# Expert gate and up weights loaded and awaited in two halves of four row blocks

## The chip, the cores and the metric

The kernel runs on one core of a Trainium2 chip. The metric is device time in microseconds (us) of one execution of the whole program. Three executions of the kernel before gave 1589.13, 1584.79 and 1586.37 us; the median is 1586.37.

## What is computed

Two layers of a backbone with two streams of 128 tokens each (context and latent), 1024 wide, all in float32. Each layer has a token-mixing part (gated linear attention, a convolution module and neighbourhood attention, joined by an output projection) and a mixture-of-experts part, the one that the change touches:

```python
scores = jax.nn.sigmoid((t @ router_w).astype(jnp.float32))
...
top_e = lax.top_k(masked, TOP_K)[1]                # 8 of 64 experts for each token
...
act = jax.nn.silu(jnp.einsum('td,edf->tef', t, w_gate)) * jnp.einsum('td,edf->tef', t, w_up)
routed = jnp.einsum('tef,efd->td', act * gate[:, :, None], w_down)
```

An expert has a gate and an up matrix of 1024 x 256 and a down matrix of 256 x 1024, 1.049 MB each. The 256 tokens together reach all 64 experts, so a layer loads 192 such matrices.

## The kernel before, in words

**Passes.** The experts of a layer are ordered by load and packed into 26 passes (`WIDTHS`, lines 90 to 92; `PLACED`, line 111). A pass fills 128 token rows with four tiles of 32; an expert takes one to four of them, so a pass serves one to four experts and a layer's 26 passes serve 64. The loop over layers runs this stage twice.

**Slots and loads.** Five slots in the on-chip memory hold one expert each (four in `ring`, one in `store` and `work`, lines 431 to 435). SP, the engine that issues these transfers, goes through the passes in order (lines 560 to 573). For each expert of the pass it reads the expert's number, waits in `gate_up_free` until the slot's gate and up part is free (for all but the first five experts: until `gu_done` counts the pass that used it last), and issues two transfers (`load_gate_up`, lines 437 to 440), gate and then up. Both count on the slot's semaphore `gate_in`, 16 each. Then, for each expert of the pass, it waits in `down_free` until `Y_shown` counts the second down half of the slot's last pass and issues the down matrix (`load_down`, `down_in`). All of it is one queue in order: what stands behind a waiting issue waits too.

**Layout.** Partition p of a slot holds the eight consecutive rows 8p to 8p+7 of each matrix, 256 floats a row (`"(p k) n -> p k n"`, k = 8), gate first and then up. A row block kt is the 128 rows 8p+kt.

**TensorE (PE).** For each pass p (lines 987 to 1012) PE

1. waits for `gate_in` of all experts of the pass (lines 990, 991) and for the gathered tokens (`X_kept`, line 992);
2. runs `gate_up_pass` (lines 936 to 941): for kt from 0 to 7 and for each of the four tiles a product of 32 columns of `X_e` with 512 columns of weights (gate and up of row block kt), added up in bank 4; the last one counts `gu_done`;
3. scatters the rows of the pass before (`scatter`, line 965), turns this pass's weights and activations (lines 946, 952), gathers half of the next pass's tokens (`gather`, line 925);
4. waits for `down_in` of all experts of the pass and for `turn_kept`, runs the first half of the down products (line 958), gathers the other half of the tokens and runs the second half.

Each float32 product appears as two instructions, so `gate_up_pass` shows 64 a pass. ACT takes the gate half through Silu (line 1239) as soon as `gu_done` counts, VectorE multiplies it with the up half (line 1543), and ACT copies the turned activations (line 1241), the tokens of the next pass (line 1224) and so on.

Of the kernel before, what the change touches and what calls it, by code (L numbers as in the profile page):

```python
# [26 lines left out]
KT = D // P  # L27
# [32 lines left out]
SLOTS = len(EXPERT_SLOTS)  # L60
# [61 lines left out]
first_done first_kept first_bias""".split()  # L122

SIGNALS = """matrices bias_next small_in vec_in norm_in attn_in shared_in chunk_in0 chunk_in1 chunk_in2
gate_in0 gate_in1 gate_in2 gate_in3 gate_in4 down_in0 down_in1 down_in2 down_in3 down_in4 act_step dve_step ada_done ada_kept bias_in square_done 
mod_shown h_ready hT_shown hT_ready vec_shown vec_ready proj_done proj_kept z_shown la_log la_ready
conv_sig tap conv_ready convT_shown ctok_ready convB_shown conv_neg cact_ready pw_shown cat_conv nq_ready
kco_ready nT_shown nT_ready bias_ready scores_shown max_ready p_exp p_ready pT_shown pT_ready pv_shown cat_na
# [17 lines left out]
def expert_slot(e):  # L146
    return EXPERT_SLOTS[e % SLOTS]


def build(nc, A):  # L150
# [4 lines left out]
    s = {name: nc.alloc_semaphore(name) for name in LASTING + SIGNALS}  # L155
# [265 lines left out]
    def dma_in(eng, out, in_, sem):  # L421
        eng.dma_start(out, in_).then_inc(sem, 16)

    def pre_slot(n):
        return n % PRE_SLOTS
# [5 lines left out]
    def slot_gate_up(slot):  # L431
        return ring[:, slot, 0:2 * KT * FF] if slot < RING else slot4_gate_up
# [4 lines left out]
    def load_gate_up(eng, slot, weights, sem):  # L437
        for j, w in enumerate(weights):
            dma_in(eng, slot_gate_up(slot)[:, KT * FF * j:KT * FF * (j + 1)].rearrange("p (k n) -> p k n", k=KT),
                   w.rearrange("(p k) n -> p k n", k=KT), sem)  # L440

    def load_down(eng, slot, w, sem):
        dma_in(eng, slot_down(slot).rearrange("p (j n) -> p j n", j=2), w.rearrange("(p j) n -> p j n", j=2), sem)

# [18 lines left out]

    chunk_in = [s["chunk_in0"], s["chunk_in1"], s["chunk_in2"]]
    gate_in = [s["gate_in0"], s["gate_in1"], s["gate_in2"], s["gate_in3"], s["gate_in4"]]
    down_in = [s["down_in0"], s["down_in1"], s["down_in2"], s["down_in3"], s["down_in4"]]
    N_SMALL, N_VEC, N_ATTN = 18, 8, 2 * HEADS + 2

    layers = nc.Fori(0, DEPTH)
    layer = layers.__enter__()  # L470
    following = (layer + 1) % DEPTH
    with nc.Block() as block:
        @block.sync
        def _(sp):
            dma_in(sp, gbc[:], A["norm_mix"][bass.ds(layer, 1), :].partition_broadcast(P)[:, 0, :], s["norm_in"])

            for n in range(PRE):
                if n >= PRE_SLOTS:
                    chunk_used(sp, n - PRE_SLOTS)
                slot = ring[:, pre_slot(n), :]  # L480
                sem = chunk_in[pre_slot(n)]
# [78 lines left out]
            for p in range(PASSES):  # L560
                wave = [k for k in range(EXPERTS) if EXPERT_PASS[k] == p]
                e = {}
                for k in wave:
                    r = LOADED[k][1]
                    e[k] = sp.value_load(order_i[0:1, r:r + 1], min_val=0, max_val=EXPERTS - 1)
                    gate_up_free(k)
                    load_gate_up(sp, expert_slot(k),
                                 [A[w][layer, bass.ds(e[k], 1)][0] for w in ("exp_w_gate", "exp_w_up")],
                                 gate_in[expert_slot(k)])
                for k in wave:  # L570
                    down_free(k)
                    load_down(sp, expert_slot(k), A["exp_w_down"][layer, bass.ds(e[k], 1)][0],
                              down_in[expert_slot(k)])
# [42 lines left out]
        def _(pe):  # L616
# [63 lines left out]
            for c in range(2):  # L680
                last = nc.tensor.transpose(bank(5, 64 * c, 64 * c + R_END), vec[:, P * c:P * (c + 1)],
                                           ident[0:R_END, 0:R_END])
# [12 lines left out]
            for st in range(STREAMS):  # L695
                for c in range(2):
                    at = 256 * st + P * c
                    last = nc.tensor.transpose(bank(4, at, at + P), cacc[:, c, st, :], ident[:])
# [8 lines left out]
            for a in range(PAIRS):  # L707
                last = nc.tensor.transpose(bank(1, P * a, P * (a + 1)), kvc[:, 0, P * a:P * (a + 1)], ident[:])
# [5 lines left out]
            for c in range(2):  # L714
                for st in range(STREAMS):
                    at = 256 * c + P * st
                    last = nc.tensor.transpose(bank(5, at, at + P), cTok[:, st, P * c:P * (c + 1)], ident[:])
# [4 lines left out]
            for e in range(2):  # L722
                r = slice(DK * e, DK * (e + 1))
                for a in range(PAIRS):
                    last = mm(bank(e, P * a, P * (a + 1)), qnT[r, a, 0:P], knT[r, a, 0:P], start=True, stop=True)
            last.then_inc(s["scores_shown"], 1)
            for e in range(2):
                r = slice(DK * e, DK * (e + 1))
                for a in range(PAIRS):
# [3 lines left out]
                    last = mm(bank(2 + e, 256 * a + P, 256 * (a + 1)), qnT[r, a, P:2 * P], kcT[r, a, :],  # L733
                              start=True, stop=True)
# [4 lines left out]
            for o in range(2):  # L739
                for c in range(2):  # L740
                    last = mm(bank(4, 256 * o, 256 * (o + 1)), wpw[:, c, P * o:P * (o + 1)],
                              cacc[:, c, :, :].rearrange("p s t -> p (s t)"), start=(c == 0), stop=(c == 1))
# [6 lines left out]
            for i, block_in in enumerate(blocks):  # L749
                last = nc.tensor.transpose(bank(1 + i // 4, P * (i % 4), P * (i % 4 + 1)), block_in, ident[:])  # L750
# [54 lines left out]
            for e in range(2):  # L805
                for a in range(PAIRS):
# [6 lines left out]
                    last = mm(out1, kvc[:, 1, DK * hh:DK * (hh + 1)], pT[:, HEADS + 2 * i + 1, :],  # L813
                              start=False, stop=True)
# [115 lines left out]
            def tiles(p):  # L930

                k0 = EXPERT_PASS.index(p)
                return [(TILE * (first + i), expert_slot(k0 + c))
                        for c, (r, first, w) in enumerate(PLACED[p]) for i in range(w)]

            def gate_up_pass(b, tiles):
                for kt in range(KT):
                    for first, slot in tiles:
                        last = mm(ps[first:first + TILE, 4, :], X_e[:, b, kt, first:first + TILE],  # L939
                                  gate_up(slot, kt), start=(kt == 0), stop=(kt == KT - 1))  # L940
                return last
# [45 lines left out]
            for p in range(PASSES):  # L987
                q = p % 2
                used = [EXPERT_PASS.index(p) + c for c in range(len(PLACED[p]))]
                for k in used:  # L990
                    pe.wait_ge(gate_in[expert_slot(k)], 32 * (k // SLOTS + 1))
                pe.wait_ge(s["X_kept"], 2 * p + 2)
                gate_up_pass(q, tiles(p)).then_inc(s["gu_done"], 1)
                if p:
                    pe.wait_ge(s["Y_kept"], 2 * p)
                    scatter().then_inc(s["scattered"], 1)
                pe.wait_ge(s["S_ready"], p + 1)
                turn_weights()
                pe.wait_ge(s["act_done"], p + 1)
                turn_acts().then_inc(s["turned"], 1)  # L1000
                if p + 1 < PASSES:
                    pe.wait_ge(s["G_ready"], p + 2)
                    gather(6, G[1 - q], 0).then_inc(s["X_shown"], 1)
                for k in used:
                    pe.wait_ge(down_in[expert_slot(k)], 16 * (k // SLOTS + 1))
                pe.wait_ge(s["turn_kept"], p + 1)
                down_pass(tiles(p), 0).then_inc(s["Y_shown"], 1)
                if p + 1 < PASSES:
                    pe.wait_ge(s["X_kept"], 2 * p + 3)
                    gather(6, G[1 - q], 1).then_inc(s["X_shown"], 1)  # L1010
                pe.wait_ge(s["Y_kept"], 2 * p + 1)
                down_pass(tiles(p), 1).then_inc(s["Y_shown"], 1)
# [685 lines left out]
```

## Time and profile before

| what | value |
|---|---|
| median of three executions | 1586.37 us |
| the profiled execution, its own time | 1593.01 us |
| its span, first to last instruction | 1591.3 us |
| mean granted TensorE clock over the span | 0.966 of full speed |
| PE busy | 1463.2 us (92%) |
| HBM read | 505.49 MB, 319 GB/s over the span |
| weights of the experts, both layers | 384 transfers of 1024 KB |

The page gives times in microseconds. PE is TensorE's products, PEld its weight loads (which overlap the products), DVE is VectorE, ACT is ScalarE, SP the engine that issues most transfers. The span is also shown in 40 equal slices, with one digit for the busy share of each engine in tenths. A view of windows gives, for stretches of the span, the busy time and number of instructions of each engine, the granted clock of TensorE, the share of the 16 DMA engines that was busy (a little over 1 where packets overlap) and the rate. A row of the timeline gives the start, the duration, and in brackets the idle time before with what ended it. In the view of waits the columns are the total, the number of waits and the longest.

### The profile page before, as it was taken

To read this page: it belongs to the slowest core of one execution; us is meant where nothing else is said; L and a number is where in the kernel's file an instruction comes from. 1 tells how busy PE (TensorE), PEld (TensorE's weight loads), DVE (VectorE), ACT (ScalarE), POOL (GpSimd) and SP (SyncE) were. 2 spreads that over 40 slices of the span, in tenths; PEclk is the share of its full clock that TensorE was granted. 3 is DMA by queue.
4 is the path that set the end of the run, shared out by engine and by line. 5 is a ranking of instruction groups with operands and counts; after the bars stand their busy time and mean duration, and the time that the engine had idled before them with its cause. 6 is when DMAs were issued, how large, how long until landed. Compare 5 with 4: busy or idle time off the path is not lost. (4 is left out here: it accounts for less than half of the span.)

```text
span 1591.3 us, 28207 instructions
## 1 busy us (share of the span) xinstructions
PE 1463.2 (92%) x12120; PEld 781.4 (49%) x12121; DVE 459.7 (29%) x956; ACT 260.0 (16%) x441; POOL 107.1 (7%) x349
## 2 busy tenths in 40 slices
PE   4899989899999998999959999889999999999996
PEld 3665765644434443434436667564443444344442
DVE  2291784501111110111133639571111111111112
ACT  1223211511111110111113131041111111111110
POOL 2600430000000000000000016000000000000000
PEclk8999989899999999999989999989999999999999
DMA  7755960399999999999944678207999999999994
GB/s 252 257 181 190 334 218 1 134 421 420 421 421 406 400 422 397 421 420 420 374 158 137 245 260 309 87 1 327 421 420 416 421 421 420 419 400 421 419 421 178
DMA packets 109252, 509.56 MB, mean 320 GB/s; under 512 B 12864, under 2 KB 14652, under 8 KB 59196
## 3 DMA queue, kind: packets, MB, share of 16 engines
q1 hardware_dynamic: 108508, 506.52, 79.4%
q8 instruction: 100, 1.64, 0.4%
q0 software_dynamic: 384, 1.05, 0.2%
q14 instruction: 36, 0.29, 0.1%
q10 hardware_dynamic: 224, 0.06, 0.0%
HBM read 505.49 MB, written 2.10 MB: 319 GB/s over the span
## 5 line engine op out<-in xcount | busy, mean ns | idle before, releaser
L939 PE MATMUL ps<-ring,h 128*32 128x512 f32 x2720 | 375.4, 601 | 25.5 <-DMA ring<-in_exp_w_up 15.0
L939 PEld LDWEIGHTS ps<-ring,h 128*32 128x32 f32 x2720 | 110.3, 111 | 248.9 <-issue 248.9
L958 PE MATMUL ps<-ring,work 128*32 128x512 f32 x1360 | 199.6, 598 | 3.1 <-DVE store L1545 1.6
L939 PE MATMUL ps<-store,h 128*32 128x512 f32 x608 | 189.9, 615 | 9.0 <-issue 5.4
L965 PE MATMUL ps<-store,work 128*128 128x512 f32 x416 | 192.4, 605 | 1.6 <-DVE store L1553 1.6
L925 PEld LDWEIGHTS ps<-tm,work 128*128 128x128 bf16 x2496 | 144.4, 98 | 44.3 <-issue 43.1
L925 PE MATMUL ps<-tm,work 128*128 128x128 bf16 x2496 | 156.9, 219 | 0.3
L1543 DVE TENSOR_TENSOR work<-work,ps 128x256 f32<-128x256 f32 x52 | 21.9, 422 | 410.7 <-ACT work L1239 410.7
L965 PEld LDWEIGHTS ps<-store,work 128*128 128x128 f32 x416 | 74.7, 189 | 120.0 <-issue 116.5
L1545 DVE COPY store<-ps 128x512 f32<-128x512 f32 x52 | 36.0, 692 | 328.9 <-PE ps L958 328.9
L673 PE MATMUL ps<-ring,store 128*128 128x512 f32 (+1 forms) x256 | 101.3, 555 | 0.0
L958 PE MATMUL ps<-work 128*32 128x512 f32 x304 | 99.2, 598 | 0.0
L1239 ACT ACTIVATE work<-ps 128x256 f32<-128x256 f32 x52 | 20.0, 384 | 481.8 <-PE ps L939 481.8
L1224 ACT COPY h<-ps 128x512 f32<-128x512 f32 x104 | 61.0, 587 | 177.3 <-PE ps L925 177.3
L319 PE MATMUL ps<-ring,cs 128*32 128x128 f32 x1792 | 60.3, 291 | 17.7 <-DMA ring<-in_w_ada 17.7
L958 PEld LDWEIGHTS ps<-ring,work 128*32 128x32 f32 x1360 | 42.3, 109 | 69.4 <-issue 56.8
L622 PE MATMUL ps<-store,pick 128*128 128x128 f32 x384 | 54.1, 307 | 22.0 <-issue 10.2
L673 PEld LDWEIGHTS ps<-ring,store 128*128 128x128 f32 x256 | 49.3, 195 | 48.7 <-issue 46.8
L670 PE MATMUL ps<-store,ring 128*128 128x256 f32 (+1 forms) x288 | 66.9, 393 | 2.2 <-ACT store L1073 2.2
L939 PEld LDWEIGHTS ps<-store,h 128*32 128x32 f32 x608 | 47.7, 113 | 39.9 <-issue 39.9
L622 PEld LDWEIGHTS ps<-store,pick 128*128 128x128 f32 x384 | 52.8, 222 | 28.2 <-issue 22.1
L607 POOL TENSOR_TENSOR store<-h,work 128x64 f32<-128x64 f32 x196 | 57.2, 333 | 132.0 <-PE ps L813 95.4
(276 smaller groups left out, 1316.8 us busy)
## 6 DMA issues: line engine op xcount, KB each, us to landing
ring<-in_exp_w_gate SPq DMA_DIRECT2D x102, 1024.0 KB, 15.0
ring<-in_exp_w_up SPq DMA_DIRECT2D x102, 1024.0 KB, 17.2
ring<-in_exp_w_down SPq DMA_DIRECT2D x102, 1024.0 KB, 15.5
ring<-in_w_ada SPq DMA_DIRECT2D x28, 2048.0 KB, 10.4
store<-in_exp_w_gate SPq DMA_DIRECT2D x26, 1024.0 KB, 15.0
store<-in_exp_w_up SPq DMA_DIRECT2D x26, 1024.0 KB, 17.1
work<-in_exp_w_down SPq DMA_DIRECT2D x26, 1024.0 KB, 14.8
ring<-in_w_in SPq DMA_DIRECT2D x6, 2048.0 KB, 13.0
```

Of the source, the lines that this page charges most:

```text
L319: last = nc.tensor.matmul(out[32 * c:32 * (c + 1), :], cs[:, kt, :], w[:, kt, P * c:P * (c + 1)], start=(kt == 0), stop=(kt == KT - 1))
L607: last = tt(*views, ALU.mult)
L622: last = mm(bank(b, P * c, P * (c + 1)), pick[:, c, st, :], ada[:, n, :], start=True, stop=True)
L670: last = mm(ps[0:w, b, 0:STREAMS * P], wt[:, kt, :], hT[:, kt, :], start=(kt == 0), stop=(kt == KT - 1))
L673: last = mm(bank(b, 0, w), hT[:, kt, P * st:P * (st + 1)], wt[:, kt, :], start=(kt == 0), stop=(kt == KT - 1))
L925: last = mm(bank(X_bank, P * k, P * (k + 1)), hs[:, part, st, KT // 2 * half + k, :], onehot[:, st], start=(st == 0 and part == 0), stop=( ...
L939: last = mm(ps[first:first + TILE, 4, :], X_e[:, b, kt, first:first + TILE], gate_up(slot, kt), start=(kt == 0), stop=(kt == KT - 1))
L958: last = mm(ps[first:first + TILE, 7, :], turn[:, P * j + first:P * j + first + TILE], down(slot, j, half), start=(j == 0), stop=(j == 1))
L965: last = mm(bank(2 * st + half), turn[:, FF + P * st:FF + P * (st + 1)], Y[:, 512 * half:512 * (half + 1)], start=False, stop=False, skip_ ...
L1224: return nc.scalar.copy(X_e[:, b, KT // 2 * half:KT // 2 * (half + 1), :], bank(6).rearrange("p (k n) -> p k n", n=P))
L1543: tt(acts[:, 0, :], silu[:, 0, :], bank(4, FF, 2 * FF), ALU.mult).then_inc(s["act_done"], 1)
L1545: nc.vector.tensor_copy(Y[:, 0:512], bank(7)).then_inc(s["Y_kept"], 1)
```

## The change

`load_gate_up` of the routed experts is replaced by two calls of a new `load_part`, one for row blocks 0 to 3 and one for 4 to 7. An expert's gate and up matrices come in four transfers: gate first half, up first half, gate second half, up second half. The second halves count on five new semaphores, `rest_in`. `gate_up_pass` takes a range of row blocks; a pass waits for the first halves of all its experts, runs the products of blocks 0 to 3, waits for the second halves of all its experts, and runs blocks 4 to 7. The last product counts `gu_done` as before. The waits on `X_kept` move ahead of those on the weights. `load_down`, the slots, the order of experts, the shared expert and the path for left-over tokens stay as they were.

```diff
+    HALF_KT = (slice(0, KT // 2), slice(KT // 2, KT))
+
+    def load_part(eng, slot, weights, kts, sem):
+
+        for j, w in enumerate(weights):
+            dma_in(eng, slot_gate_up(slot).rearrange("p (a k n) -> p a k n", a=2, k=KT)[:, j, kts, :],
+                   w.rearrange("(p k) n -> p k n", k=KT)[:, kts, :], sem)
...
                     gate_up_free(k)
-                    load_gate_up(sp, expert_slot(k),
-                                 [A[w][layer, bass.ds(e[k], 1)][0] for w in ("exp_w_gate", "exp_w_up")],
-                                 gate_in[expert_slot(k)])
+                    for kts, half_in in zip(HALF_KT, (gate_in, rest_in)):
+                        load_part(sp, expert_slot(k),
+                                  [A[w][layer, bass.ds(e[k], 1)][0] for w in ("exp_w_gate", "exp_w_up")],
+                                  kts, half_in[expert_slot(k)])
...
-            def gate_up_pass(b, tiles):
-                for kt in range(KT):
+            def gate_up_pass(b, tiles, kts=range(KT)):
+                for kt in kts:
...
-                for k in used:
-                    pe.wait_ge(gate_in[expert_slot(k)], 32 * (k // SLOTS + 1))
                 pe.wait_ge(s["X_kept"], 2 * p + 2)
-                gate_up_pass(q, tiles(p)).then_inc(s["gu_done"], 1)
+                for kts, half_in in zip(HALF_KT, (gate_in, rest_in)):
+                    for k in used:
+                        pe.wait_ge(half_in[expert_slot(k)], 32 * (k // SLOTS + 1))
+                    last = gate_up_pass(q, tiles(p), range(kts.start, kts.stop))
+                last.then_inc(s["gu_done"], 1)
```

## Rows read from the trace of the kernel before

**Rows 1.** The page: busy time of the engines; then DMA in 40 slices.

```profile
PE 1463.2 (92%) x12120; PEld 781.4 (49%) x12121; DVE 459.7 (29%) x956; ACT 260.0 (16%) x441; POOL 107.1 (7%) x349
...
DMA  7755960399999999999944678207999999999994
GB/s 252 257 181 190 334 218 1 134 421 420 421 421 406 400 422 397 421 420 420 374 158 137 245 260 309 87 1 327 421 420 416 421 421 420 419 400 421 419 421 178
```

**Rows 2.** DMA view of the first expert stage, 305 to 790 us.

```profile
DMA packets 27605, 201.38 MB, mean 415 GB/s; under 512 B 3056, under 2 KB 3056, under 8 KB 3056
```

**Rows 3.** Timeline of PE in the first layer: starts of passes, the last pass.

```profile
377.71 0.60 PE L939 MATMUL ps<-ring,h 128*32 128x512 f32 x3
...
394.73 0.61 PE L958 MATMUL ps<-ring,work 128*32 128x512 f32 x3
...
395.15 7.05 PE L939 MATMUL ps<-ring,h 128*32 128x512 f32 x64
...
453.44 1.08 PE L939 MATMUL ps<-store,h 128*32 128x512 f32 x3 [3.57 <-issue]
...
784.35 0.63 PE L939 MATMUL ps<-ring,h 128*32 128x512 f32 x3 [1.09 <-DMA store<-in_exp_w_up]
...
796.28 0.63 PE L958 MATMUL ps<-ring,work 128*32 128x512 f32 x3 [0.77 <-ACT work L1241]
```

**Rows 4.** Waits of PE over the span: total us, times, longest us.

```profile
PE ps L939 <- DMA ring<-in_exp_w_up: 18.6, 8, 4.3
...
PE ps L939 <- issue: 13.5, 8, 3.6
```

**Rows 5.** Windows: stretches of the two expert stages; clock, DMA share, GB/s last.

```profile
513.00:519.00 6.00, 6.00 (x36) 2.20 (x29) 0.42 (x1) 0.38 (x1) 0.00 (x0) 1.00 0.75 289
544.00:550.00 6.00, 5.41 (x52) 2.06 (x56) 0.52 (x1) 0.00 (x0) 0.00 (x0) 1.00 0.86 315
620.00:628.00 8.00, 7.56 (x76) 2.54 (x71) 0.69 (x1) 0.13 (x1) 0.00 (x0) 1.00 0.81 302
...
1394.00:1402.00 8.00, 7.56 (x73) 2.54 (x76) 0.80 (x2) 0.59 (x1) 0.00 (x0) 1.00 0.85 308
...
792.00:794.00 2.00, 2.00 (x6) 0.84 (x5) 0.32 (x1) 0.00 (x0) 0.00 (x0) 1.00 0.14 57
...
450.00:460.00 10.00, 6.56 (x36) 1.86 (x40) 0.63 (x1) 0.00 (x0) 0.00 (x0) 0.66 1.02 423
```

**Rows 6.** DMA view of 16:24, 829:832, 46:49, 26:27, 390:430 us, in that order.

```profile
DMA packets 1519, 3.10 MB, mean 387 GB/s; under 512 B 17, under 2 KB 17, under 8 KB 1517
...
DMA packets 395, 1.21 MB, mean 404 GB/s; under 512 B 0, under 2 KB 0, under 8 KB 395
...
DMA packets 407, 1.25 MB, mean 417 GB/s; under 512 B 0, under 2 KB 0, under 8 KB 407
...
DMA packets 126, 0.40 MB, mean 401 GB/s; under 512 B 9, under 2 KB 9, under 8 KB 126
...
DMA packets 2308, 16.82 MB, mean 420 GB/s; under 512 B 258, under 2 KB 258, under 8 KB 258
```

**Rows 7.** DMA issues of the whole span: count, KB each, us to landing.

```profile
ring<-in_exp_w_down SPq DMA_DIRECT2D x102, 1024.0 KB, 15.5
...
ring<-in_sh_w_gate SPq DMA_DIRECT2D x2, 1024.0 KB, 6.2
```

**Rows 8.** Timeline of SP: two issues of one expert.

```profile
772.94 0.34 SPq L422 DMA_DIRECT2D store<-in_exp_w_gate  x1
773.37 0.38 SPq L422 DMA_DIRECT2D store<-in_exp_w_up  x1
```

**Rows 9.** Waits of SP over the span: total us, times, longest us.

```profile
SPq L422 <- PE ps L958: 332.8, 40, 9.0
SPq L422 <- PE ps L939: 331.6, 47, 14.2
```

More of the change, by code:

```diff
@@ L124 @@
 SIGNALS = """matrices bias_next small_in vec_in norm_in attn_in shared_in chunk_in0 chunk_in1 chunk_in2
-gate_in0 gate_in1 gate_in2 gate_in3 gate_in4 down_in0 down_in1 down_in2 down_in3 down_in4 act_step dve_step ada_done ada_kept bias_in square_done
+gate_in0 gate_in1 gate_in2 gate_in3 gate_in4 rest_in0 rest_in1 rest_in2 rest_in3 rest_in4 down_in0 down_in1 down_in2 down_in3 down_in4 act_step dve_step ada_done ada_kept bias_in square_done
 mod_shown h_ready hT_shown hT_ready vec_shown vec_ready proj_done proj_kept z_shown la_log la_ready
@@ L465, in build @@
     gate_in = [s["gate_in0"], s["gate_in1"], s["gate_in2"], s["gate_in3"], s["gate_in4"]]
+    rest_in = [s["rest_in0"], s["rest_in1"], s["rest_in2"], s["rest_in3"], s["rest_in4"]]
     down_in = [s["down_in0"], s["down_in1"], s["down_in2"], s["down_in3"], s["down_in4"]]
```

## The prediction, made before the changed kernel was run

> **What bounds the kernel now.** I read the page first. Over the span PE is busy 92%, but in the two long plateaus of the slices (the ninth to the 20th and from the 29th on, the expert stages of the two layers) the DMA line stands at 9 and the GB/s line near 420 in nearly every slice [rows 1]. Two engines near full: the question is which ends last. The traffic answers. One layer loads 64 experts of three 1.049 MB matrices, 201.3 MB, and the DMA view of the first stage, 305 to 790 us, counts 201.38 MB at a mean of 415 GB/s [rows 2]. The stage lasts as long as these bytes take. PE, by the timeline, needs 17.45 us for a pass that waits for nothing (377.71 to 395.15) [rows 3]: 26 passes are 453.7 us against 479.3 us for 201.3 MB at 420 GB/s. So the expert stage is bound by the weight stream, and PE sits out most of the difference ahead of line 939, 18.6 and 13.5 us over both layers [rows 4]. The 13.5 put to "issue" are of the same kind: the 3.57 us before 453.44 lie at the first product of a pass, where the gate wait stands [rows 3].
>
> The stream itself is nearly gapless. It runs dry in four places: 289 GB/s over 6 us, 315 over 6, 302 over 8, 308 over 8 [rows 5]. Against 420 that is 1.9 + 1.5 + 2.2 + 2.1 = 7.7 us of lost stream in both layers. There SP stood at a slot that PE had not freed. These 7.7 us are all that an earlier PE can win from the middle of a stage.
>
> **The change part by part.** *Earlier start of a pass (removes).* Of an expert's four transfers the last two carry 1.049 MB, 2.5 us at 420 GB/s. The 64 products of line 939 take 7.05 us [rows 3], so half of them (3.5 us) cover 2.5: a pass that waits today starts up to 2.5 us earlier and, if the stream is on time, waits no more in its middle. In a stream-bound stage this does not shorten the stage by 2.5 us a pass, since the next bytes come no sooner; what is late next is the next expert's weights. It wins in two places only. (a) Slots come free earlier, so the dry places shrink. Of 7.7 us I take 7, because the stream also gets slower (below), which lets PE catch up. (b) The last pass of a layer starts earlier against the end of the stream. Today it starts at 784.35, its down products start at 796.28 after ACT (line 1241), and the last bytes land between 792 and 794 [rows 3, 5]. About 2 us after that landing are all that can go, as the down products would then wait for down_in instead. Two layers: -4 us.
>
> *Smaller packets (adds).* A partition reads 8 rows of 256 floats, 8192 contiguous bytes, of each matrix; with half the row blocks it reads 4096. In 390 to 430 us the view counts 2308 packets, 258 of them small, so 2050 carry 16.82 MB: 8.2 KB each, 420 GB/s [rows 6]. No stretch has 4096 alone at length, so I bound its rate by neighbours in size. Column chunks of w_ada (2 KB) ran at 387 GB/s, of w_in (3 KB) at 404 in one stretch and 417 in another, a stretch mostly of the 4 KB rows of x at 401 [rows 6]. One engine's time for a packet is its bytes over a sixteenth of the rate: 84.7 ns (2048), 121.7 (3072 at 404), 117.9 (3072 at 417), 312.1 (8192). Lines to 8192 give for 4096: 160.5 ns (408 GB/s), 159.8 (410) and 156.7 (418). Gate and up are 134.2 MB a layer: 319.5 us at 420, 328.1 at 409, 321.1 at 418, 334.7 at 401. I take 409, because the two stretches behind it come after some microseconds of saturated queues, as the expert stage does, and 417 stands at the start of one: +8.6 us a layer, +17.2 in both. Ends: +3.2 and +30.4.
>
> The Trainium skill has a measured load stream of 1 MiB transfers with 4 KiB rows, 408.7 GB/s on a core alone (DMA: Bandwidth & Descriptors, iDMA fabric); with it the term would be +17.7, and no run here shows that stream yet.
>
> *More transfers (adds).* 128 more a layer. Each ends in one small packet per engine (3056 in 305 to 790 us for 192 transfers, 16 each) [rows 2]. The line from 2048 to 8192 has a constant of 84.7 - 75.8 = 8.9 ns a packet; 128 of them are 1.1 us a layer, +2.3 in both. Below: nothing, if it overlaps. Above: an idle stretch at each transfer; the only long row is a 1 MB transfer on an empty queue, which lands after 6.2 us [rows 7] against 2.5 us of bytes, but in 390 to 430 us 16 transfers of 1.049 MB fill 40 us at 420 GB/s [rows 6], so a queued transfer pays none of it.
>
> The Trainium skill states against this change that a transfer costs about 2.0 us plus its bytes over 436 GB/s and asks for 1 MiB or more in each (DMA: Bandwidth & Descriptors, Anatomy of one DMA and Rules for kernel authors). By that, 256 more would add 512 us; the same rule would put a 1 MB transfer at 4.4 us, and the trace disagrees with its 2.5 us a transfer in a full queue.
>
> *SP's queue.* Each expert has two more issues of about 0.43 us (772.94 to 773.37) [rows 8]: 55 us a layer, hidden in SP's own waits of 332.8 and 331.6 us behind lines 958 and 939 [rows 9]. Queued behind them are the value loads and down issues of the same pass, up to 0.9 us later per expert; the backlog covers that (down transfers land 15.5 us after issue) [rows 7]. Without that cover, in a dry place, the first transfer still goes out at the same moment. Nothing.
>
> *PE's queue.* Up to four waits stand between the two halves; behind them are the second half, scatter, turn and the gathers, and ACT (line 1239) waits for them. Met waits cost nothing visible: the step from 394.73 to 395.15 crosses several waits and takes 0.42 us, as any other [rows 3]. Even a whole step of 0.42 us at each would be 10.9 us of PE time a layer, under the 25.6 by which the stream is longer (479.3 - 453.7).
>
> *Clock.* After the idle time before 453.44 a stretch was granted 0.66 on average, part at 1.2 and part at 2.4 GHz, and its first products took 1.08 us where others take 0.61 [rows 3, 5]. A shorter idle may keep it up; that is PE time too, and already in (a).
>
> **Sum.** 17.2 + 2.3 - 7 - 4 = +8.5 us. The profiled execution took 1593.0 us (span 1591.3), so 1601.5; the median of the runs shown is 1586.4, 6.6 lower, and the difference moves over: 1594.9.
>
> **Rivals.** *A. A 4 KB packet costs nothing more.* If gate and up keep 418 GB/s or better, as one 3 KB stretch suggests [rows 6], the stream grows by 3.2 + 2.3, and the early start decides: all 7.7 us of dry places and the two tails go: -6.2 us, 1580.2; with no added cost at all -11.7, 1574.7. Its place is the packet rate of the expert stage, and it turns the sign from about 414 GB/s up (134.2 MB there take 324.2 us, +9.4 in both layers, and 2.3). Against it: two stretches in three lie lower. Chance 0.18.
> *B. The loss is near 401 GB/s*, the row for x [rows 6]: +30.4 + 2.3 - 11 = +21.7, 1608.1. Against it: that stretch has 2 KB packets mixed in. Chance 0.12.
> *C. The new wait takes the place of the old.* The stream is late, so PE starts on the first halves and then stands in the middle; slots are freed no earlier, and the down weights of the last pass end the layer: nothing is won, 19.5 us is lost, 1605.9. For it: a pass that starts 2.5 us early still needs the same last byte. Against it: 3.5 us of products cover 2.5 us of bytes. Chance 0.10.
> *D. Loss and gain cancel*: 413 to 415 GB/s, where the stream loses 7.8 to 10.9 us with 2.3 more and wins 11: within 3 us, 1586. Chance 0.20.
> *E. Each added transfer pays idle time* (6.2 - 2.5 = 3.7 us, 256 times, +947 us): excluded by the full stretches except for 0.01.
>
> **How the numbers follow.** My forecast (408 to 410 GB/s, 1593 to 1598) has 0.39. What a measurement of this kernel can tell from no change is about 0.3%, 4.8 us. Slower by more: most of the forecast, B, C, E and a little of D, 0.60. Faster by more: most of A and a little else, 0.17. Within: D and what A and the forecast leave, 0.23. The range leaves out the far end of A, half of B and E: 1579 to 1608.
>
> **What would show it right or wrong.** Right: in the expert stages the DMA share stays full, packets under 8 KB grow by 65,536 over the run, and the rate is 408 to 413 GB/s where it is 420 now; the dry places are mostly gone; the stages grow by some 5 us each; idle time before line 939 does not go down in sum but comes earlier or splits in two. Wrong: a rate of 418 or more in full stretches (A), a rate near 401 (B), dry places of the same size and standing in mid-pass (C).

## The result, and the profile after

The changed kernel took 1606.22 us (median of four runs, 1605.42 to 1616.38); the kernel before, beside it, 1587.75 us (four runs, 1584.79 to 1591.06). The ratio of all runs is 1.013, with a 95% interval of 1.0085 to 1.0176 (that of the two medians is 1.0116): by the medians 18 us slower, where 8.5 were forecast. Timed again in the company of other kernels it stood at 1607.92 against 1589.92, 1.0115 (1.0096 to 1.0133). The profiled executions, 1593.01 and 1606.05, lie 13.0 apart, because the one of before is 5 us above its median.

Where the time went is read best from the starts of the expert passes in PE's timeline (first product of line 939 before, 949 after):

| stretch, us | before | after |
|---|---|---|
| start to pass 0 of layer 1 | 325.9 | 323.5 |
| pass 0 to pass 25, layer 1 | 458.4 | 463.6 |
| pass 25 to pass 0 of layer 2 | 318.9 | 318.2 |
| pass 0 to pass 25, layer 2 | 455.9 | 466.3 |
| pass 25 to the end | 32.2 | 32.8 |
| span | 1591.3 | 1604.4 |

The growth is in the two expert stages, +15.6 us; the first row differs before the change has done anything. Next the rate of the stream. First the page of after (PE, DMA slices, GB/s, packets), to be held against [rows 1]:

```profile
PE 1462.7 (91%) x12120; PEld 779.1 (49%) x12121; DVE 459.5 (29%) x956; ACT 259.5 (16%) x441; POOL 106.6 (7%) x349
...
DMA  6755950499999999999844778109999999999994
GB/s 249 258 182 204 336 192 0 169 413 412 413 406 411 414 411 392 411 413 412 359 173 141 268 259 307 38 1 373 413 412 413 412 412 402 412 394 413 395 412 198
DMA packets 146124, 509.65 MB, mean 318 GB/s; under 512 B 16960, under 2 KB 18748, under 8 KB 128828
```

Most slices of the plateaus stand at 411 to 414 where [rows 1] has 420 to 422. Packets under 8 KB were 59,196 before, so 69,632 came: 65,536 halves of 8 KB rows, and 16 end packets for each of 256 added transfers. The DMA view of after, 390 to 430 us, against the last row of [rows 6]:

```profile
DMA packets 3860, 16.46 MB, mean 411 GB/s; under 512 B 428, under 2 KB 428, under 8 KB 3281
```

A full stretch runs at 411 GB/s, not 420, and some 70% of the bytes in this one came in 4 KB packets (of the whole stage two thirds do). Does PE now wait in mid-pass? The timeline of PE after, at pass 15 and at the last pass of layer 1:

```profile
602.13 1.07 PE L949 MATMUL ps<-ring,h 128*32 128x512 f32 x2 [4.67 <-DMA ring<-in_exp_w_up]
...
610.96 1.01 PE L949 MATMUL ps<-ring,h 128*32 128x512 f32 x3
...
787.00 0.63 PE L949 MATMUL ps<-ring,h 128*32 128x512 f32 x3 [1.37 <-DMA store<-in_exp_w_up]
...
799.41 0.63 PE L968 MATMUL ps<-ring,work 128*32 128x512 f32 x3 [1.25 <-DMA work<-in_exp_w_down]
```

The idle time in brackets stands at the first product of a pass, as in [rows 3]. In all 52 passes no step between two products of one pass is longer than 0.43 us at full clock, 0.81 in passes at a lower one. The last row answers to the row at 796.28 in [rows 3]: the down products of the last pass now wait for the weights themselves, 1.25 us. Waits of PE over the span, against [rows 4]:

```profile
PE ps L949 <- DMA ring<-in_exp_w_up: 36.0, 14, 5.4
PE ps L949 <- DMA store<-in_exp_w_up: 8.2, 4, 3.2
PE ps L968 <- DMA work<-in_exp_w_down: 2.6, 2, 1.4
PE ps L968 <- DMA ring<-in_exp_w_down: 2.3, 3, 1.0
```

Idle time ahead of gate and up products is 44.2 us; before it was 34.4 (18.6, 13.5 and 2.3 for `store`). And windows of after: first the four dry places of [rows 5], then the stretches that are thin now, then pass 15 (PEclk, DMA share and GB/s are the last three columns):

```profile
513.00:519.00 6.00, 6.00 (x48) 3.43 (x50) 0.40 (x1) 1.17 (x2) 0.00 (x0) 1.00 1.03 410
544.00:550.00 6.00, 5.09 (x48) 1.92 (x52) 0.00 (x0) 0.00 (x0) 0.00 (x0) 1.00 1.02 419
620.00:628.00 8.00, 8.00 (x85) 2.84 (x86) 1.45 (x5) 0.58 (x1) 0.00 (x0) 1.00 0.91 348
1394.00:1402.00 8.00, 8.00 (x70) 4.48 (x67) 1.03 (x2) 1.55 (x3) 0.00 (x0) 1.00 1.02 409
...
455.00:470.00 15.00, 15.00 (x138) 7.10 (x132) 1.78 (x4) 2.14 (x4) 0.00 (x0) 1.00 1.01 394
618.00:634.00 16.00, 16.00 (x140) 6.66 (x133) 2.54 (x6) 1.45 (x4) 0.00 (x0) 1.00 0.96 357
1328.00:1338.00 10.00, 10.00 (x75) 4.20 (x68) 0.42 (x1) 0.56 (x2) 0.00 (x0) 1.00 0.98 365
1400.00:1416.00 16.00, 15.86 (x137) 6.53 (x126) 2.54 (x6) 1.09 (x4) 0.00 (x0) 1.00 0.97 363
1500.00:1510.00 10.00, 10.00 (x76) 4.40 (x69) 0.42 (x1) 0.83 (x2) 0.00 (x0) 1.00 0.98 348
...
602.00:612.00 10.00, 9.87 (x65) 2.74 (x65) 0.00 (x0) 0.00 (x0) 0.00 (x0) 0.71 1.02 418
```

At three of the four old windows the stream is full, but the dry places have moved rather than gone. The five stretches that are thin now lose 0.6 + 2.1 + 1.1 + 1.9 + 1.5 = 7.2 us of stream at 411 (9.8 in six stretches of its repeated run, below), against 7.7 before. They also look different: the DMA share is 0.96 to 1.01 there, where the old dry places had 0.75 to 0.86, so what brings the rate down is more that packets take longer than that none are there; why was not settled. The last row shows the price of a long wait: after 4.67 us idle the pass ran at 0.71 of full clock on average, part at 1.2 and part at 2.4 GHz, and took 9.86 us instead of 7.05. It is not a new price: before, the same pass waited 4.30 us and took 9.33.

### The profile page after: what moved, and what is told of

Its sections match the earlier page's. It is cut to its first block and busy times, and to the rows that moved or that the text cites. A ratio compares the mean times of both kernels' runs of the same rounds, so it can differ in the third digit from the quotient of the medians.

```text
span 1604.4 us, 28909 instructions
## 1 busy us (share of the span) xinstructions
PE 1462.7 (91%) x12120; PEld 779.1 (49%) x12121; DVE 459.5 (29%) x956; ACT 259.5 (16%) x441; POOL 106.6 (7%) x349
## 5 line engine op out<-in xcount | busy, mean ns | idle before, releaser
L683 PE MATMUL ps<-ring,store 128*128 128x512 f32 (+1 forms) x256 | 97.9, 540 | 0.0
L319 PE MATMUL ps<-ring,cs 128*32 128x128 f32 x1792 | 59.6, 289 | 18.6 <-DMA ring<-in_w_ada 18.6
## 6 DMA issues: line engine op xcount, KB each, us to landing
ring<-in_w_in SPq DMA_DIRECT2D x6, 2048.0 KB, 13.5
```

The costliest lines, as they stand in the source:

```text
L319: last = nc.tensor.matmul(out[32 * c:32 * (c + 1), :], cs[:, kt, :], w[:, kt, P * c:P * (c + 1)], start=(kt == 0), stop=(kt == KT - 1))
L683: last = mm(bank(b, 0, w), hT[:, kt, P * st:P * (st + 1)], wt[:, kt, :], start=(kt == 0), stop=(kt == KT - 1))
```

## The experiments

Each kernel was timed beside the kernel before on one chip. "Joined" means that a pass waits for all of its gate and up weights. The idle column is the time that PE waited ahead of gate and up products in the profiled run, both layers; waits for down weights (4.9 us in the changed kernel, 1.5 to 4.2 in the other split ones, none with a joined wait) are not in it. The rows come from several chips. For a comparison of two rows the ratios are the safer guide, and where two intervals overlap the difference is open.

| kernel | packets | wait | median, us | ratio to before (95%) | idle, us |
|---|---|---|---|---|---|
| before (profiled run) | 8 KB | joined | 1588 to 1590 | 1 | 34.4 |
| whole transfers | 4 KB | joined | 1608.1 | 1.0107 (1.0090 to 1.0124) | 44.7 |
| the same, cut by every other partition | 4 KB | joined | 1611.2 | 1.0135 (1.0114 to 1.0156) | 43.8 |
| halves, gate gate up up | 4 KB | joined | 1615.0 | 1.0171 (1.0147 to 1.0196) | 51.3 |
| halves, gate up gate up | 4 KB | joined | 1622.1 | 1.0202 (1.0185 to 1.0218) | 56.3 |
| **changed** | 4 KB | split | 1606.2 | 1.0130 (1.0085 to 1.0176) | 44.2 |
| halves, gate gate up up | 4 KB | split | 1611.8 | 1.0132 (1.0115 to 1.0149) | 43.7 |
| whole transfers | 4 KB | split | 1603.2 | 1.0087 (1.0074 to 1.0100) | 41.8 |
| whole transfers | 8 KB | split | 1588.2 | 0.9985 (0.9974 to 0.9996) | 29.9 |

### Head start away, halves kept

```diff
-                for kts, half_in in zip(HALF_KT, (gate_in, rest_in)):
-                    for k in used:
-                        pe.wait_ge(half_in[expert_slot(k)], 32 * (k // SLOTS + 1))
-                    last = gate_up_pass(q, tiles(p), range(kts.start, kts.stop))
+                for k in used:
+                    pe.wait_ge(gate_in[expert_slot(k)], 32 * (k // SLOTS + 1))
+                    pe.wait_ge(rest_in[expert_slot(k)], 32 * (k // SLOTS + 1))
+                gate_up_pass(q, tiles(p)).then_inc(s["gu_done"], 1)
```

> Loads in halves as changed, but a pass waits for both halves before its first product. Packet theory (the expert stage is bound by the weight stream, 4 KB packets of gate and up slow it, the head start wins back only the two tails and part of the dry places): slower than before by 20 to 28 us, that is 2 to 10 us slower than the changed kernel, with the same rate of about 411 GB/s in full stretches. Rival, the wait in the middle of a pass costs the time: faster than the changed kernel, near before. Rival, the head start is worth nothing: the same as the changed kernel within 2 us.

Measured: 1622.07 us against 1589.99, +32 us, more than the 20 to 28 expected. Run again on another chip, because its first expert stage had also begun some 4 us later than in other kernels:

> The kernel of the joined wait once more, unchanged: halves loaded as in the changed kernel, all four waited for before the pass. Theory (the halves themselves cost 11 to 14 us beside their packet size): 1620 to 1624 again, idle before the gate and up products about 28 us a layer. Rival (a part was an accident of that chip, as the 4 us more before its first expert stage suggest): 1612 to 1618.

1623.5 against 1589.49, ratio 1.0204 (1.0178 to 1.0229). The 32 us hold. The changed kernel run again beside other experiments stands at +18:

> The changed kernel again, beside the three others on one chip: slower than before by 14 to 20 us on any theory.

So the head start is worth 14 us in the changed kernel, and what it sits on costs 32. The waits of PE with the joined wait:

```profile
PE ps L949 <- DMA ring<-in_exp_w_up: 46.3, 16, 6.3
PE ps L949 <- DMA store<-in_exp_w_up: 10.0, 5, 2.7
```

### 4 KB packets alone

A slot is laid out half by half, so that each 1 MB transfer writes and reads pieces of 4 KB; count of transfers and waits are those of before.

```diff
+                        dma_in(sp, slot_gate_up(expert_slot(k)).rearrange("p (h a k n) -> p a h (k n)", h=2, a=2, k=KT // 2)[:, j],
+                               A[w][layer, bass.ds(e[k], 1)][0].rearrange("(p h k) n -> p h (k n)", h=2, k=KT // 2),
+                               gate_in[expert_slot(k)])
```

> As before in transfers (128 of 1 MB a layer) and waits, but the halves of gate and up lie interleaved in a slot, so that each transfer is made of 4 KB packets. Packet theory: full stretches at 408 to 412 GB/s, slower than before by 17 to 25 us. Rival, the number of transfers is what costs: the same as before within 4 us at 420 GB/s.

Measured: 1608.13 against 1589.99, +18 us. The DMA view of 390 to 430 us, then the waits of PE:

```profile
DMA packets 3724, 16.44 MB, mean 411 GB/s; under 512 B 246, under 2 KB 246, under 8 KB 3194
```
```profile
PE ps L940 <- DMA ring<-in_exp_w_up: 27.2, 10, 3.6
PE ps L940 <- issue: 11.6, 8, 2.3
PE ps L940 <- DMA store<-in_exp_w_up: 5.9, 2, 3.1
```

The packet size alone gives the rate of the changed kernel and a loss as large as its whole loss. A stretch of this kernel in which every packet is of 4 KB or less gives the price directly, the DMA view of 680 to 692 us:

```profile
DMA packets 1273, 4.90 MB, mean 408 GB/s; under 512 B 77, under 2 KB 77, under 8 KB 1273
```

At 408 instead of 420 GB/s the 134.2 MB of gate and up of a layer take 328.9 us instead of 319.5, +18.8 in both layers, close to the 18 measured.

### The number of transfers, at 8 KB and at 4 KB

Three kernels add transfers to the kernel before and keep its packets: two transfers a matrix, of the lower and the upper 64 partitions; two transfers of every other partition; and two added transfers of 128 bytes for each expert.

```diff
+                        for lo in (0, P // 2):
+                            dma_in(sp, slot_gate_up(expert_slot(k))[lo:lo + P // 2, KT * FF * j:KT * FF * (j + 1)],
...
+                        for odd in range(2):
+                            dma_in(sp, slot_gate_up(expert_slot(k))[odd::2, KT * FF * j:KT * FF * (j + 1)],
...
+                    for j in range(2):
+                        dma_in(sp, spare[lo:lo + 16, c0:c0 + 2], A["x_prompt"][0, lo:lo + 16, c0:c0 + 2], s["spare_in"])
```

> As before in packets (8 KB) and waits, but each gate and up matrix comes in two transfers of 64 partitions: 128 more transfers a layer, on the same semaphore. Packet theory: the same as before, at most 4 us slower (one more small packet per engine and transfer), 418 to 420 GB/s in full stretches. Rival, the number of transfers is what costs (idle time at each, SP's issues): slower than before by 12 to 20 us.

> Packets of 8 KB and waits as before, but each gate and up matrix in two transfers of every other partition: twice the transfers, the same packets, all parts of the on-chip memory in each. Theory that the number of transfers costs (about 14 us lie between the run with joined waits and the run with small packets in whole transfers): slower than before by 8 to 16 us at 420 GB/s in full stretches. Theory that transfers are nearly free and the 14 us come from small packets and transfers together: within 4 us of before. If 64 partitions are slow however they are chosen: slower by hundreds of us, as in the run with lower and upper partitions.

> As before, with two added transfers of 128 bytes (16 partitions, 8 bytes each) per expert into a spare tile: 128 more transfers a layer that bring no bytes worth counting. Theory that a transfer costs by itself: slower than before by 8 to 16 us. Rival, a transfer costs only its small packets (two rounds of some 9 ns per engine each, 2.3 us a layer): slower by 2 to 6 us.

Measured: 2347.39 against 1589.99 for the lower and upper halves, 1.4722 (1.4665 to 1.4779); 1591.2 against 1589.92 for every other partition, 1.0009 (0.9996 to 1.0021); 1590.23 for the empty ones, 1.0012 (0.9998 to 1.0026). The first is a cost of its own kind (last section). The other two show that 128 more transfers a layer cost little or nothing here at 8 KB: 1.3 and 0.3 us by the medians, some 4 at the ends of the intervals (both theories had expected more of the empty ones). The same cut on 4 KB packets:

> The layout and the waits of the kernel with 4 KB packets in transfers of 1 MB, each transfer cut in two of every other partition: 4 KB packets, and as many transfers as the changed kernel, 0.5 MB each, with one joined wait ahead of the pass. It differs from the kernel of joined halves only in which rows a transfer holds. Theory (many transfers of small packets cost what joined halves cost, 14 us above the 4 KB packets alone): about 1622. Rival (the count of transfers is free at 4 KB as it was at 8 KB, and the 14 us of joined halves come from the order in which the quarters of a slot are fetched, half a row of gate, half a row of up, then the other halves): about 1608.

1611.2 against 1588.24, 1.0135: its interval overlaps that of 4 KB packets alone, and it lies 11 us below the joined halves (1.0185 to 1.0218), which have as many transfers of as many packets. The number of transfers is not the main part of what makes the halves dear.

### What is left: half rows, and the order of the halves

```diff
-                    for kts, half_in in zip(HALF_KT, (gate_in, rest_in)):
+                    for j, (w, sem) in enumerate((("exp_w_gate", gate_in), ("exp_w_up", rest_in))):
+                        for kts in HALF_KT:
```

> The kernel of the joined wait with its four half transfers issued gate, gate, up, up in place of gate, up, gate, up. Theory (what the halves add comes from the order, the pieces of two matrices in turn): about 1609, as with every other partition. Rival (it comes from transfers that hold half of every row, whatever their order): about 1622, as with the joined wait before.

1614.97 against 1589.49, 1.0171 (1.0147 to 1.0196): between the two forecasts, and this does not decide between them. Its interval overlaps that of the joined halves in the other order (1.0185 to 1.0218, again 1.0178 to 1.0229) and that of every other partition (1.0114 to 1.0156); only the 4 KB packets alone (1.0090 to 1.0124) lie clear of it. By the medians, of the 14 us that joined halves cost above 4 KB packets some 7 go with the order gate, up, gate, up; that share is not shown.

Where the 14 us are lost can be seen in part. The rate of the joined halves in a full stretch, 390 to 430 us, is 412 GB/s, no lower than that of the whole transfers. Over a whole stage it is lower. The DMA views of 430 to 790 and 1110 to 1560 us, whole transfers of 4 KB packets first, then the joined halves:

```profile
DMA packets 31956, 146.71 MB, mean 408 GB/s; under 512 B 2234, under 2 KB 2234, under 8 KB 25910
DMA packets 40153, 183.83 MB, mean 409 GB/s; under 512 B 2796, under 2 KB 2796, under 8 KB 32693
```
```profile
DMA packets 33150, 145.14 MB, mean 403 GB/s; under 512 B 3682, under 2 KB 3682, under 8 KB 27232
DMA packets 41822, 183.24 MB, mean 407 GB/s; under 512 B 4639, under 2 KB 4639, under 8 KB 34330
```

In equal time the halves bring 1.57 and 0.59 MB less, 5.2 us of stream at 411 (in the run repeated on another chip 8.4), of the 7.7 us (11.9) by which these profiled expert stages are longer from pass 0 to pass 25. So halves waited for together make the stream run thin more often. The changed kernel, which is the same but for the split wait, has 409 and 408 GB/s in these windows. Idle time of PE goes the same way: 44.7, 43.8, 51.3 and 56.3 us down the table. Why half rows make the stream thin was not settled.

### What a head start is worth elsewhere

With whole transfers the gate matrix comes first, so PE can run the gate products (256 columns) before it waits for up.

```diff
+                for j, part_in in enumerate((gate_in, rest_in)):
+                    for k in used:
+                        pe.wait_ge(part_in[expert_slot(k)], 16 * (k // SLOTS + 1))
+                    last = part_pass(q, tiles(p), j)
```

> Whole 1 MB transfers with 8 KB packets as before; a pass waits for the gate matrices, runs the gate products of all eight row blocks with 256 columns each, then waits for the up matrices and runs theirs. The same head start of one 1 MB transfer (2.5 us) without smaller packets. Packet theory: faster than before by 4 (tails) to 11 us (tails and dry places), unless the 256-column products take PE longer than the 512-column ones; the rate in full stretches stays at 420 GB/s. Rival, the split wait itself costs: slower than before by 5 us or more at an unchanged rate.

> Whole 1 MB transfers of 4 KB packets (1608, +18 on before, with the old wait), and gate products that wait for the gate matrix alone. Theory (nothing is lost here that a head start could repay but its 2 us at 8 KB and the tails): 1604 to 1608. Rival (a head start is worth 14 us where the stream carries 4 KB packets): about 1594.

> Halves of 4 KB packets issued gate, gate, up, up, and gate products that wait for the two gate halves alone, up products after them for the two up halves. It stands to the kernel with the same order and a joined wait (1615, +27 on before) as the changed kernel stands to the joined wait in its own order. Theory (a head start repays what the halves cost beside their packet size, and little beyond): it falls to the level of 4 KB packets alone, 1605 to 1609. Rival (it is worth 14 us whenever the stream carries 4 KB packets): about 1601.

Measured: 1588.16 against 1589.99 at 8 KB, 0.9985, which is less than the 4 to 11 us expected; 1603.21 against 1588.83 with whole transfers of 4 KB packets, 5 us below the same without a head start (1604 to 1608 was the theory); 1611.8 against 1588.83 with halves in the order gate, gate, up, up, 3 us below, where 1605 to 1609 was the theory. A head start is worth 2 to 5 us by the medians (the intervals of the two 4 KB pairs overlap) and 14 only where halves in the order gate, up, gate, up had lost about as much. The products of 256 columns do not hide a gain: a pass that waits for nothing takes 7.11 us with them and 7.07 without.

Releasing the gate part of a slot as soon as the gate products end, with all gates of a pass issued ahead of its ups, was slower:

> Whole 1 MB transfers of 8 KB packets; all gate matrices of a pass come ahead of its up matrices, a pass runs all gate products and then all up products, and the gate part of a slot is free for the next expert after the gate products. If what is left of the dry places comes from slots that are freed late in passes of four experts: 3 to 10 us faster than before, rate 420 GB/s with fewer dry stretches. If the stream has no more to give: the same as the run with gate and up awaited in turn, 1 to 3 us faster than before.

1595.4 against 1589.92, 1.0035 (1.0022 to 1.0049). With all gates first, a pass of four experts has its ups last, and the waits moved into the middle of its passes, up to 3.5 us: the second wait of rival C, in a kernel made for it.

### Are the dry places worth anything?

In SP's timeline of before a down issue at 440.45 is followed by the next only at 449.93, and gate and up issues whose slots were free stand behind it. Two orders of issue were tried: every load in the order in which its slot comes free, and one gate and up pair ahead of each down issue that has to wait.

```diff
+            for part, k in sorted(wanted_order, key=lambda item: freed(*item)):
...
+                if part and freed(k) > shown:
+                    shown = freed(k)
+                    ahead = next((i for i in range(at, len(line)) if not line[i][0]), None)
+                    if ahead and freed(line[ahead][1]) <= shown:
+                        line.insert(at, line.pop(ahead))
```

> The kernel before with SP's 192 weight issues in another order: each stands where its slot comes free (gate and up of an expert by the end of the gate and up products of the pass that held the slot, the down weights by that pass's second Y), not wave by wave. Nothing is split; packets and counts stay. Theory (after a pass of four experts the stream runs thin because gate and up issues whose slots are free stand behind a down issue that waits for Y_shown, and only there does an earlier release pay): the thin stretches of before (513:519, 544:550, 620:628, 1394:1402) fill up, the stream's length goes from 490 to about 484 us and the time falls by 5 to 10 us, to some 1580. Rival (the thin stretches are short of free slots, whatever the order of issue): within 3 us of the kernel before.

> The order of issue of the kernel that issues as slots come free, and the head start in 8 KB packets: gate products wait for the gate matrix alone, up products wait after them. Theory: both gains add, since the order fills the stream after passes of four and the head start lets a pass begin some 2.4 us (one 1 MB transfer) sooner: 1 to 3 us below the kernel with the order alone, some 1578. Rival (a head start only moves the wait, the stream sets the end): equal to the kernel with the order alone within 1.5 us.

> The changed kernel with the same order of issue. Theory (the changed kernel pays about 17 us for its 4 KB packets all along the stream, and its gain at the dry places never came because the free slots' issues stand behind the waiting down issues): the order gains as much as on the kernel before or more, 5 to 12 us, 1596 to 1602, still above the kernel before. Rival (its extra idle time comes from SP's blocked issues, longest 6 us with the queues full): the order changes little or makes it worse, 1606 to 1612.

Measured against 1588.24: 1625.46 (1.0230), 1622.68 (1.0201) and 1642.58 (1.0333, the changed kernel in this order). My theory fell. The waits of PE in the first, from 300 to 800 us:

```profile
PE ps L962 <- issue: 16.9, 4, 4.9
PE ps L943 <- DMA ring<-in_exp_w_up: 12.8, 2, 9.0
```

Line 962 is the down products: up to four gate and up pairs go ahead of the down weights of the next pass, and PE stands up to 4.9 us for these (the longest wait ends at 569.93, when down weights have landed at 569.84), a wait that [rows 4] does not have. Line 943 is the gate and up products, where one pass waited 9.0 us.

> The kernel before, whole transfers, with one change of order: ahead of a down issue that would be the first to wait for a pass's second Y, SP issues the gate and up of one more expert, whose slot is free by then. Theory (the dry places come from free slots behind a waiting down issue; three gates ahead made the down weights 5 us late, one gate ahead leaves them in time): the thin stretches at 620:628 and 1394:1402 fill, 3 to 7 us less than before, some 1583. Rival (any gate ahead delays down weights that a pass waits for at L958, or the thin stretches are short of slots): 0 to 10 us more than before.

> The same order of issue, and gate products that wait for the gate matrix alone. Theory: 1 to 3 us below the kernel with one gate ahead, some 1581, the fastest of all here. Rival (the head start moves the wait only): equal to it within 1.5 us.

Measured: 1588.08 against 1589.49, 0.9988 (0.9975 to 1.0000); with the split wait 1589.69, 1.0004 (0.9988 to 1.0020). The four dry places of [rows 5] in the first of these, then its waits of PE:

```profile
513.00:519.00 6.00, 6.00 (x77) 3.81 (x79) 1.36 (x3) 1.76 (x3) 0.00 (x0) 1.00 1.01 422
544.00:550.00 6.00, 6.00 (x48) 1.90 (x41) 0.42 (x1) 0.38 (x1) 0.00 (x0) 1.00 1.01 415
620.00:628.00 8.00, 8.00 (x62) 3.72 (x52) 0.42 (x1) 0.97 (x2) 0.00 (x0) 1.00 1.01 420
1394.00:1402.00 8.00, 8.00 (x77) 2.37 (x70) 0.69 (x1) 0.02 (x1) 0.00 (x0) 1.00 1.02 421
```
```profile
PE ps L968 <- DMA ring<-in_exp_w_down: 19.1, 8, 3.9
PE ps L949 <- DMA ring<-in_exp_w_up: 12.1, 7, 2.1
```

All four places are full, and the time is lower by 1.4 us by the medians, with an interval that ends at no change. But this does not show that the order filled them. Dry places lie elsewhere in another execution: in this one other stretches are thin, the first two rows below among them, 4.7 us of stream at 420 in all. The kernel with the empty transfers, which issues its loads in the order of before, is as full at the old places (the next two rows; the others of them stand at 421 and 422), thin beside them (the last row), and loses 3.8 us in all:

```profile
767.00:772.00 5.00, 5.00 (x27) 2.19 (x20) 0.42 (x1) 0.38 (x1) 0.00 (x0) 1.00 0.86 333
1288.00:1293.00 5.00, 5.00 (x25) 1.90 (x18) 0.42 (x1) 0.38 (x1) 0.00 (x0) 1.00 0.87 321
```
```profile
620.00:628.00 8.00, 8.00 (x52) 3.00 (x45) 0.42 (x1) 0.38 (x1) 0.00 (x0) 1.00 1.00 411
1394.00:1402.00 8.00, 8.00 (x60) 2.63 (x51) 0.29 (x1) 0.38 (x1) 0.00 (x0) 0.86 1.01 421
615.00:621.00 6.00, 5.52 (x55) 1.81 (x56) 0.87 (x3) 0.59 (x1) 0.00 (x0) 1.00 0.84 320
```

What filled dry places are worth stays open. The wait for gate and up shrank from 34.4 to 13.1 us (12.1 and 1.0 for `store`), and 19.1 us of waiting for down weights took its place. The best ratio of all kernels here is the 0.9985 (0.9974 to 0.9996) of gate then up at 8 KB, 2 us by the medians.

## Why the prediction was right and wrong

**The direction, right, and for its reason.** The stream bounds the stage, and smaller packets slow it. The packets term was +17.2, from 409 GB/s for 4 KB packets; a stretch of 4 KB packets alone runs at 408, and the kernel with nothing but these measured +18. The prediction named 408.7 from the Trainium skill (DMA: Bandwidth & Descriptors, iDMA fabric); the trace agrees, with 408.

**The step that failed: the dry places, -7 ("Slots come free earlier, so the dry places shrink").** They moved and did not shrink: 7.2 us (9.8 in the repeated run) lost in thin stretches, 7.7 before. The time from a layer's first weight issue to its last landing was to grow by 17.2 + 2.3 - 7 = 12.5 us in both layers; it grew by 20.7 (490.0 to 497.5 and 487.3 to 500.5; 24.0 in the repeated run). Less the 4 us of the tails this is some 17, near the 18 measured. The 7.7 us were also read off a single execution, 5 us above its median: the kernel with the empty transfers, whose loads are those of before, loses 3.8. And with one gate and up pair issued ahead, the wait removed at the gate products came back at the down products.

**Behind it: "More transfers (adds)", +2.3.** It priced the 128 added transfers of a layer by their small end packets, and looked at nothing but their number. The number is indeed nearly free (+1.3 and +0.3 us at 8 KB, within the intervals). The Trainium skill (DMA: Bandwidth & Descriptors, Anatomy of one DMA) gives a transfer 2.0 us beside its bytes, and states it for transfers that GpSimd issues, which the prediction left out; the 256 empty ones, issued by SP into a queue that is nearly always at work, would have cost 512 us by it and cost 0.3. But cutting the slot into halves of rows, fetched gate, up, gate, up, cost 14 us above the small packets with a joined wait (1622.1 against 1608.1), 5 to 8 of them seen as a thinner stream. What a partition's row is cut into, and in which order the pieces of one slot arrive, was not costed at all. The earlier start won this back, and so had nothing left for the dry places.

**The tails, -4, as forecast.** The last bytes of layer 1 landed at 799.2 and the down products began at 799.41; before, 794.1 and 796.28 [rows 3]: the gap of 2.2 us became 0.25, 1.9 us a layer, and `down_in` is the next wait, as the text said.

**By measured terms** the sum is 18 (packets) + 14 (halves) - 14 (split wait, tails included) = +18. The prediction had 17.2 + 2.3 - 11 = 8.5. That 14 is near 11 is luck: the 11 were to come on top of an undisturbed stream.

**Rivals.** A fell (411 GB/s, not 418). B named 1608.1 and came within 2 us of the time, but by luck: its rate of 401 for 4 KB packets no full stretch shows (408). C fell in its mechanism: no wait stands in mid-pass and the tails were won, although the idle time grew (34.4 to 44.2) and the dry places kept their size, as it said. D fell with A. E fell with the empty transfers.

**Smaller steps.** The page's count of packets came as said (65,536 and the end packets). SP's two added issues were put at 0.43 us each and hidden in its waits; in fact SP now stands in the issues themselves. One row of SP's timeline of after, then its waits over the span, against [rows 8] and [rows 9]:

```profile
574.95 5.09 SPq L422 DMA_DIRECT2D ring<-in_exp_w_up  x1
```
```profile
SPq L422 <- PE ps L968: 137.8, 28, 8.4
SPq L422 <- PE ps L949: 122.0, 27, 10.9
```

Its waits on PE fell by 405 us, and issues that took 0.34 to 0.38 us in [rows 8] (1.4 at most) take up to 6.1. Whether that costs anything was not tried by itself; 4 KB packets in whole transfers show it too, and their loss is what their rate explains.

## What to carry to other kernels

Where a stage is bound by its weight stream, first ask what an earlier start does to the transfers: here 4 KB rows instead of 8 KB cost 3% of the rate (408 against 420 GB/s, 18 us), and no kernel with 4 KB rows came back to zero. If a pass may start on a part, let the part be a whole matrix, so that packets stay as they are (gate first, then up: 0.9985). A wait removed in one place can come back at the next, here at the down weights. Dry places in the stream move with every change and differ between executions: sum them over the whole stage, not where they were.

## What the runs showed that was not expected

- A transfer of 64 adjacent partitions runs at little more than half the rate, one of every other partition at full rate, both with 8 KB rows and equal counts. The DMA view of 390 to 430 us of the two, adjacent first:

```profile
DMA packets 1456, 9.76 MB, mean 244 GB/s; under 512 B 267, under 2 KB 267, under 8 KB 267
```
```profile
DMA packets 2499, 16.81 MB, mean 420 GB/s; under 512 B 450, under 2 KB 450, under 8 KB 450
```

- Four pieces of one slot that hold half rows, all waited for together, cost up to 14 us more than whole rows of the same packets, at an equal rate in full stretches. Their order moved the medians by 7 us (1615.0 to 1622.1), with intervals that overlap.
- A joined wait of halves made one pass of the first layer wait 6.3 us, where whole transfers of the same packets waited 3.6 at most; the passes that follow waits of such length ran partly at the lower clock (0.71 of full clock on average after 4.67 us in the changed kernel).
